# Four gate projections of the merge as filling work in the last delta head's scan, in place of two ahead of it

## Chip, cores and metric

The kernel runs on one core of one Trainium2 chip. The metric is the device time of one execution, in microseconds. Its engines here: PE (TensorE), DVE (VectorE), ACT (ScalarE), POOL (GpSimd) and SP (SyncE, which here only issues transfers). Each runs its own instructions strictly in order, and they wait for one another through semaphores.

## What is computed

One transformer block over 512 tokens of width 1024, with 256 context tokens ahead of them: a feed-forward sublayer, a mixer and a second feed-forward sublayer. The mixer has eight attention heads and eight gated delta-rule heads; both run over chunks and are merged:

```python
def step(s, xs):
    q_d, k_d, u_c, w_c, a_c, d_c = xs
    v_new = u_c - jnp.einsum('bhcd,bhde->bhce', w_c, s)
    o = jnp.einsum('bhcd,bhde->bhce', q_d, s) + jnp.einsum('bhij,bhje->bhie', a_c, v_new)
    s = s * d_c[..., None, None] + jnp.einsum('bhcd,bhce->bhde', k_d, v_new)
...
def _merge(o_dn, z, o_at, gates, dn_norm, w_dn_out, w_attn_out, w_out):
    o = _rmsnorm(jnp.swapaxes(o_dn, 1, 2), dn_norm).astype(z.dtype)
    o = o * jax.nn.silu(z.reshape(b, l, DN_HEADS, DN_DV))
    y_dn = o.reshape(b, l, DN_V) @ w_dn_out
    y_at = o_at @ w_attn_out
    g_dn, g_at = jnp.split(gates, 2, axis=-1)
    return (jax.nn.sigmoid(g_dn) * y_dn + jax.nn.sigmoid(g_at) * y_at) @ w_out
```

## The kernel before

Everything is held transposed: 128 features on the partitions, tokens along the row. A projection to 128 output features is one block `Blk(base, it, j)`: eight k tiles, and each product of fp32 numbers as three matmuls on numbers split in a high and a low part (hi x hi, lo x hi, hi x lo), 24 matmuls for the 512 tokens. Weights come by SP's transfers into a ring of four buffers `raw`. ACT rounds a block to `w_hi` (L954, `split`), DVE subtracts to get `w_lo` (L1784, `split_next`; for one block of each delta head POOL does, L869); `w_hi` and `w_lo` have two places, by the block's parity. A block's result lies in the PSUM bank of its parity (`bank`), and PE may overwrite it when `psum_read` says that it has been read. PE's count `gemm_done` grows with each finished block.

The attention outputs `o_at` and then the delta outputs `o_dn` (eight rows of 512 each, one for a head) are operands of the merge, so they are split as well: ACT rounds (`oat_hi` L1538, `odn_hi` L1706), DVE subtracts (`oat_lo` L2416, `odn_lo` L2649).

The eight delta heads run one after the other (`dn_head`, written for each engine; heads 1 to 6 are a loop, the last is written out with `final` set). On PE a head is: products of keys; projections; transposes; then, behind the inverse of the 16 x 16 diagonal blocks on DVE (L2518, L2522), which go out and back by transfers as `d_xc` (four issued by SP at L743, two by ACT at L1644) and are spread to `d_x` (L2545) in three groups, the solver: nine steps of `mid` and `grow` (L2713, out of `d_qu`), each with a copy `d_qu` on ACT (L1652) and a masked product `d_w` on DVE (L2561, L2573); then the scan over six chunks in two directions: `from_keys` (PE `d_st,d_c`), residual `d_rhs` on DVE (L2581), `solve` (PE `d_rhs,d_w`), `d_vn` on ACT (L1664), `to_state` (PE `d_vn,d_kd`), new state `d_st` on DVE (L2589, L2591), and beside them `out_state` (L3315) and `out_values` (PE `d_at,d_vn`). At its end DVE copies `d_o` (L2450).

In heads 0 to 6 the scan holds pieces of the next head's projections, of 384 columns each: `fill(n)` puts n matmuls there. The last head has none:

```python
def fill(n):
    if not final:
        piece(b[6], next_value, n)
```

Its blocks b[4] and b[5] are the two gates of the merge's first output tile. PE does 21 of b[5]'s 24 matmuls ahead of the solver and 3 before the last `grow`. ACT takes their sigmoids (`gate`, L1586) into `m_s`. Before each change between Ln/Exp, Silu and Sigmoid it loads the set of tables in which they are; the kernel asks for some of these loads (`preload_act_table_set`, L1624, L1636, L1660, L1703), others stand ahead of an instruction of their own (L1575, L1577, L1586).

Behind the scan the last head's output is normed: square, sum of squares on PE (`out_sum`, between attention rows 2 and 3 of the first merge projection, `attended`), Ln and Exp on ACT (`out_root`, L1575, L1577), `out_rows` on DVE. Then come `odn` and the merge loop: 8 output tiles of 4 blocks, gate of attention, gate of delta, attention, delta. The first tile lacks its two gates, so 7 tiles run in a loop of 96 matmuls. The matmuls of all of these are recorded on L2709.

## Time and profile before

| | |
|---|---|
| median of 3 runs | 1856.89 us (1856.65 to 1859.82) |
| profiled execution, its own time | 1859.1 us |
| its span | 1857.4 us |
| PE, DVE, ACT, POOL busy | 97%, 67%, 52%, 22% of the span |
| last delta head | about 1193 to 1251 us |
| merge loop (7 tiles) | 1270.7 to 1423.1 us |

Times in the rows are microseconds from the span's start. PE's busy share counts pipelined matmuls from start to end, which overlap, so it says little of how full PE is; the idle times in brackets, and the granted clock, say more.

### The profile page before, as it was taken

To read this page: it belongs to the slowest core of one execution; us is meant where nothing else is said; L and a number is where in the kernel's file an instruction comes from. 1 tells how busy PE (TensorE), PEld (TensorE's weight loads), DVE (VectorE), ACT (ScalarE), POOL (GpSimd) and SP (SyncE) were. 2 spreads that over 40 slices of the span, in tenths; PEclk is the share of its full clock that TensorE was granted. 3 is DMA by queue.
4 is the path that set the end of the run, shared out by engine and by line. 5 is a ranking of instruction groups with operands and counts; after the bars stand their busy time and mean duration, and the time that the engine had idled before them with its cause. 6 is when DMAs were issued, how large, how long until landed. Compare 5 with 4: busy or idle time off the path is not lost.

```text
span 1857.4 us, 31438 instructions
## 1 busy us (share of the span) xinstructions
PE 1792.7 (97%) x11197; PEld 1662.5 (90%) x11197; DVE 1239.0 (67%) x2451; ACT 956.9 (52%) x1912; POOL 401.2 (22%) x296
## 2 busy tenths in 40 slices
PE   8899999999998999999999999979999989999997
PEld 5899999999997889989999999967888989898897
DVE  7768787878667665567677787755334576376576
ACT  6534242424447655566556766644223565374463
POOL 0714141313200220023323222310000043242330
PEclk9999999999999999999999999989999999999999
DMA  8233334554231430031122222112324213233232
GB/s 331 73 119 134 122 123 141 180 175 154 88 140 41 154 102 13 1 88 52 46 67 76 65 76 65 45 38 68 99 93 169 69 47 114 70 113 103 85 131 69
DMA packets 85141, 182.86 MB, mean 98 GB/s; under 512 B 33572, under 2 KB 42916, under 8 KB 84912
## 3 DMA queue, kind: packets, MB, share of 16 engines
q1 hardware_dynamic: 79584, 167.45, 27.3%
q0 software_dynamic: 3280, 13.95, 2.3%
q8 instruction: 62, 1.02, 0.2%
q10 hardware_dynamic: 2176, 0.13, 0.1%
q14 instruction: 39, 0.32, 0.1%
HBM read 169.91 MB, written 7.39 MB: 95 GB/s over the span
## 4 chain that ended last, share of the span: by engine, by line
PE 73%; DVE 9%; ACT 6%; issue 4%; DMA 3%; SPq 3%; POOL 2%; ACTq 0%; DVEq 0%; POOLq 0%
PE ps L2709 50%; PE ps L2920 14%; PE ps L2713 3%; PE ps L3007 2%; SPq L737 2%; DMA raw<-W 1%; PE ps L3164 1%; ACT e_hi L1282 1%; DVE e_lo L2078 1%; DMA d_xc<-d_b 1%; ACT ps L1267 1%; PE ps L3315 1%; DMA d_matrices<-d_l 1%; DVE ps L2120 1%; DVE d_kc L2437 1%
## 5 line engine op out<-in xcount | busy, mean ns | idle before, releaser
L2709 PE MATMUL ps<-h_hi,w_hi 128*128 128x384 f32 (+2 forms) x720 | 240.4, 372 | 8.0 <-DVE h_lo L1854 4.1
L2709 PE MATMUL ps<-h_lo,w_hi 128*128 128x384 f32 (+2 forms) x720 | 237.0, 361 | 0.0
L2709 PE MATMUL ps<-h_hi,w_lo 128*128 128x384 f32 (+2 forms) x720 | 228.0, 356 | 0.0
L1784 DVE TENSOR_TENSOR w_lo<-raw,w_hi 128x1024 fp32r<-128x1024 f32 (+1 forms) x98 | 126.1, 1287 | 128.4 <-ACT w_hi L954 128.4
L954 ACT ACTIVATE w_hi<-raw 128x1024 fp32r<-128x1024 f32 (+1 forms) x106 | 111.4, 1051 | 153.6 <-PE ps L2709 151.7
L2709 PEld LDWEIGHTS ps<-h_hi,w_hi 128*128 128x128 f32 x720 | 130.5, 188 | 29.4 <-DVE h_lo L1854 8.2
L2709 PEld LDWEIGHTS ps<-h_lo,w_hi 128*128 128x128 f32 x720 | 133.1, 188 | 13.0 <-issue 1.2
L2709 PEld LDWEIGHTS ps<-h_hi,w_lo 128*128 128x128 f32 x720 | 133.0, 188 | 12.9
L2709 PE MATMUL ps<-g_hi,w_hi 128*128 128x384 f32 (+2 forms) x444 | 132.9, 346 | 0.8 <-DVE w_lo L1784 0.5
L2709 PE MATMUL ps<-g_lo,w_hi 128*128 128x384 f32 (+2 forms) x444 | 131.8, 343 | 0.0
L2709 PE MATMUL ps<-g_hi,w_lo 128*128 128x384 f32 (+2 forms) x444 | 131.7, 343 | 0.0
L2920 PE MATMUL ps<-h_lo,w_hi 128*128 128x384 f32 x320 | 107.0, 334 | 2.2 <-ACT pb L1212 2.2
L3007 PE MATMUL ps<-f_hi,e_hi 128*128 128x256 f32 x356 | 102.1, 287 | 6.0 <-ACT f_pb L1326 3.8
L2920 PE MATMUL ps<-h_hi,w_hi 128*128 128x384 f32 x320 | 107.3, 335 | 0.4 <-DVE ps L2008 0.3
L2920 PE MATMUL ps<-x_lo,w_hi 128*128 128x384 f32 x320 | 106.9, 334 | 0.0
L2920 PE MATMUL ps<-h_hi,w_lo 128*128 128x384 f32 x320 | 106.9, 334 | 0.0
L3007 PE MATMUL ps<-f_hi,e_lo 128*128 128x256 f32 x356 | 101.1, 284 | 0.0
L804 POOL TENSOR_TENSOR sums<-raw 128x512 f32<-128x512 f32 x20 | 28.9, 1444 | 278.6 <-DVE w_lo L1968 180.6
L2709 PEld LDWEIGHTS ps<-g_hi,w_hi 128*128 128x128 f32 x444 | 81.5, 188 | 7.4 <-DVE Y L2066 1.0
L2709 PEld LDWEIGHTS ps<-g_hi,w_lo 128*128 128x128 f32 x444 | 81.8, 188 | 5.0
L2709 PEld LDWEIGHTS ps<-g_lo,w_hi 128*128 128x128 f32 x444 | 81.7, 188 | 5.0
L1968 DVE TENSOR_TENSOR w_lo<-sums,w_hi 128x512 fp32r<-128x512 f32 x80 | 59.9, 753 | 33.8 <-ACT w_hi L1172 33.0
(479 smaller groups left out, 5134.1 us busy)
## 6 DMA issues: line engine op xcount, KB each, us to landing
raw<-W SPq DMA_DIRECT2D x221, 512.0 KB, 3.8
w_mod<-WMOD SPq DMA_DIRECT2D x68, 512.0 KB, 4.0
g_row<-g_rows POOLq DMA_DIRECT2D x8, 768.0 KB, 5.3
X<-XT SPq DMA_DIRECT2D x4, 768.0 KB, 6.9
d_matrices<-d_l SPq DMA_DIRECT2D x8, 384.0 KB, 2.8
a_sw<-i_n POOLq DMA_DIRECT2D x40, 64.0 KB, 1.9
w_first<-WMOD SPq DMA_DIRECT2D x4, 512.0 KB, 11.0
X<-XT SPq DMA_DIRECT2D x1, 2048.0 KB, 14.2
```

The costliest lines, as they stand in the source:

```text
L737: sp.dma_start(d_s[lv][r:r + b, :, col:col + b], d_l[r:r + b, 0, :, col:col + b]).then_inc(s("d_levels"), 16)
L804: g.tensor_tensor(s1[:], b1, b2, ALU.add).then_inc(s("s_add"), 1)
L954: a.activation(hi, src, ACT.Copy).then_inc(s("w_hi"), 1)
L1267: a.activation(copy_bank(pos), weight_part2(q, pos), ACT.Copy)
L1282: a.activation(slot2(True, q, pos), weight_part2(q, pos), ACT.Copy).then_inc(s("u_hi"), 1)
L1784: v.tensor_tensor(lo, src, hi.bitcast(F32), ALU.subtract).then_inc(s("w_split"), 1)
L1968: v.tensor_tensor(slot_of(w_lo, n, None), weight_part(q, pos), slot_of(w_hi, n, None).bitcast(F32), ALU.subtract)\
L2078: v.tensor_tensor(slot2(False, q, pos), src, slot2(True, q, pos).bitcast(F32), ALU.subtract).then_inc(s("u_lo"), 1)
L2709: return pe.matmul(out, lhsT, rhs, start=start, stop=stop)
L2713: return pe.matmul(out, lhsT, rhs, start=False, stop=True, skip_group_check=True)
L2920: last = pe.matmul(out_, slot_of((w_hi, w_hi, w_lo)[i], n + pos, k), (hi, lo, hi)[i][pos][:, k], start=pos in (A11, A12, S3) and k == 0 an ...
L3007: last = pe.matmul(out_, w[i][:, k], (hi, lo, hi)[i][:, k], start=pos in (A11, A12, S3) and k == 0 and i == 0, stop=True, skip_group_check ...
```

## The change

Blocks b[6] and b[7] of the last head, which were the attention and delta projection of the first tile, become the two gates of the second tile; the host puts the weight blocks in that order (`mg[0:8]`), and `merge_block` gives the place of a block in it. The four gates' results go to `m_gate`, two of them in new places.

On PE all of b[5] comes ahead of the solver, and four matmuls of b[6] behind it; `fill` puts 8, 4 or 2 gate matmuls where the other heads have 12, 5 or 3 of theirs, so that 34 stand between the last `grow` and the scan's end, and 10 behind it. On ACT the first gate is read with a Copy, and its sigmoid and the second gate follow the transfer of `d_xc`. The third gate is in step 3 of the scan, the fourth behind the scan. The attention rows are taken in the order 3 to 7, 0 to 2 (`ROWS`; the buffers of rows 0 to 2 are still in use in the scan): five are rounded in steps 1, 2 and 4 and split in steps 2, 3 and 4. The splits of the weights of the first tile's projections come in steps 3 (ACT) and 5 (DVE) and behind the scan. The second tile's projections are written out like the first's, and the merge loop has 6 tiles.

```diff
@@ -245,6 +245,16 @@
         return Blk(self.base, self.it, self.j + d)
+def merge_block(it, j):
+    if isinstance(it, int) and it < 2:
+        return Blk(B_MERGE, 0, 2 * it + j + (2 if j >= 2 else 0))
+    return Blk(B_MERGE, it, j)
+ROWS = list(range(3, H)) + list(range(3))
@@ -393,6 +403,7 @@
         m_s = at("m_s", 94, [2, SEQ])
+        m_gate = [m_s[:, 0, :], m_s[:, 1, :], at("m_s2", 98, [SEQ])[:], at("m_s3", 87.4375, [SEQ])[:]]
@@ -1533,8 +1544,8 @@
-            def round_attention(k0, k1):
-                for k in range(k0, k1):
+            def round_attention(i0, i1):
+                for k in ROWS[i0:i1]:
@@ -1581,9 +1592,9 @@
-            def gate(blk, i):
+            def gate(blk, to, bank_):
                 a.wait_ge(s("gemm_done"), blk.n + 1)
-                a.activation(m_s[:, i, :], bank(blk, 1), ACT.Sigmoid).then_inc(psum_read[blk.pair], 1)
+                a.activation(to, bank_, ACT.Sigmoid).then_inc(psum_read[blk.pair], 1)
@@ -1633,9 +1644,9 @@
                 if final:
-                    a.preload_act_table_set(SIGMOID_SET)
                     a.wait_ge(s("d_qd"), h + 1)
-                    gate(b[4], 0)
+                    a.wait_ge(s("gemm_done"), b[4].n + 1)
+                    a.activation(m_gate[0], bank(b[4], 1), ACT.Copy).then_inc(psum_read[b[4].pair], 1)
@@ -1646,6 +1657,11 @@
                     distance(h + 1, 1)
+                else:
+                    a.preload_act_table_set(SIGMOID_SET)
+                    a.wait_ge(psum_read[b[4].pair], b[4].turn + 2)
+                    a.activation(m_gate[0], m_gate[0], ACT.Sigmoid)
+                    gate(b[5], m_gate[1], bank(b[5], 1))
@@ -1655,9 +1671,6 @@
                     take(b[5])
-                else:
-                    gate(b[5], 1)
-                    a.preload_act_table_set(LOG_SET)
@@ -1666,6 +1679,13 @@
                         split(b[7])
+                    if final and t in (1, 2):
+                        round_attention(2 * t - 2, 2 * t)
+                    if final and t == 3:
+                        gate(b[6], m_gate[2], ps[:, 0, :])
+                        split(b[6].ahead(2))
+                    if final and t == 4:
+                        round_attention(4, 5)
@@ -1694,28 +1714,32 @@
                 a.activation(m_hi[:, bass.ds(it, 1), :].rearrange("p a n -> p (a n)"), m_b[:], ACT.Copy).then_inc(s("m_rounded"), 1)
+            last_gate = Blk(B_MERGE, 0, 3)
             out_square(H - 1)
-            round_attention(0, 2)
+            round_attention(5, 7)
             out_round(H - 1, 1)
-            round_attention(2, 4)
+            round_attention(7, H)
+            gate(last_gate, m_gate[3], bank(last_gate, 1))
+            split(last_gate.ahead(2))
+            a.preload_act_table_set(LOG_SET)
             out_root(H - 1)
-            round_attention(4, H)
...
                 a.activation(odn_hi[:, k], o_dn[:, k], ACT.Copy).then_inc(s("o_rounded"), 1)
-            step(Blk(B_MERGE, 0, 2))
-            step(Blk(B_MERGE, 0, 3))
-            merged(0)
+            for it in range(2):
+                step(merge_block(it, 2))
+                step(merge_block(it, 3))
+                merged(it)
...
                     if j < 2:
-                        gate(blk, j)
+                        gate(blk, m_s[:, j, :], bank(blk, 1))
                 merged(it)
-            with a.Fori(1, KT, 1) as it:
+            with a.Fori(2, KT, 1) as it:
@@ -2410,9 +2434,9 @@
-            def split_attention(k0, k1):
-                for k in range(k0, k1):
-                    v.wait_ge(s("o_rounded"), k + 1)
+            def split_attention(i0, i1):
+                for i, k in list(enumerate(ROWS))[i0:i1]:
+                    v.wait_ge(s("o_rounded"), i + 1)
@@ -2600,8 +2624,14 @@
                         pack(h + 1)
+                    if final and t in (2, 3):
+                        split_attention(2 * t - 4, 2 * t - 2)
+                    if final and t == 4:
+                        split_attention(4, 5)
...
                         out_rows(h - 1)
+                    if final and t == 5:
+                        split_next(b[6].ahead(2))
@@ -2620,23 +2650,23 @@
             dn_head(H - 1, False, True)
-            split_attention(0, 1)
+            split_attention(5, 6)
             out_add(H - 1)
-            split_attention(1, 3)
+            split_attention(6, 7)
...
             out_gain(H - 1)
-            split_attention(3, H)
+            split_attention(7, H)
+            split_next(Blk(B_MERGE, 0, 5))
...
-            def gated(blk, dst, i):
-                gate = blk.ahead(-2)
+            def gated(blk, dst, row, gate):
...
                 v.wait_ge(s("gemm_done"), blk.n + 1)
-                v.tensor_tensor(dst[:], bank(blk, 1), m_s[:, i, :], ALU.mult).then_inc(psum_read[blk.pair], 1)
-            def merged_sum(it):
-                v.wait_ge(psum_read[Blk(B_MERGE, it, 3).pair], Blk(B_MERGE, it, 3).turn + 2)
+                v.tensor_tensor(dst[:], bank(blk, 1), row, ALU.mult).then_inc(psum_read[blk.pair], 1)
+            def merged_sum(blk):
+                v.wait_ge(psum_read[blk.pair], blk.turn + 2)
@@ -2647,23 +2677,27 @@
                 v.tensor_tensor(odn_lo[:, k], o_dn[:, k], odn_hi[:, k].bitcast(F32), ALU.subtract).then_inc(s("o_split"), 1)
-            gated(Blk(B_MERGE, 0, 2), m_b, 0)
-            split_next(Blk(B_MERGE, 0, 4))
-            gated(Blk(B_MERGE, 0, 3), m_a, 1)
-            merged_sum(0)
-            step(Blk(B_MERGE, 0, 3))
-            merged_low(0)
+            for it in range(2):
+                gate = Blk(B_MERGE, 0, 2 * it + 1)
+                if it:
+                    v.wait_ge(s("m_ready"), it)
+                gated(merge_block(it, 2), m_b, m_gate[2 * it], gate)
+                split_next(merge_block(it, 2).ahead(2))
+                gated(merge_block(it, 3), m_a, m_gate[2 * it + 1], gate)
+                merged_sum(merge_block(it, 3))
+                split_next(merge_block(it, 3).ahead(2))
+                merged_low(it)
...
                     if j >= 2:
-                        gated(blk, (m_b, m_a)[j - 2], j - 2)
+                        gated(blk, (m_b, m_a)[j - 2], m_s[:, j - 2, :], blk.ahead(-2))
                     if j == 3:
-                        merged_sum(it)
+                        merged_sum(blk)
...
                 merged_low(it)
-            with v.Fori(1, KT, 1) as it:
+            with v.Fori(2, KT, 1) as it:
@@ -3173,7 +3207,7 @@
                 hi, lo, off = ((h_hi, h_lo, 0), (h_hi, h_lo, 0), (oat_hi, oat_lo, CTX), (odn_hi, odn_lo, CTX))[j]
-                gemm(Blk(B_MERGE, it, j), hi, lo, segs_x, off=off, ready=(s("o_split"), H * (j - 2)) if j >= 2 else None)
+                gemm(merge_block(it, j), hi, lo, segs_x, off=off, ready=(s("o_split"), H * (j - 2)) if j >= 2 else None)
@@ -3241,13 +3275,29 @@
+                gates = [(blk, bank_, k, i) for blk, bank_ in ((b[6], ps[:, 0, :]), (b[7], bank(b[7], 1))) for k in range(KT) for i in range(3)]
+                def gate_piece(n):
+                    for _ in range(n):
+                        blk, bank_, k, i = gates.pop(0)
+                        if k == 0 and i == 0:
+                            pe.wait_ge(s("w_split"), blk.w + 1)
+                            pe.wait_ge(psum_read[blk.pair], blk.turn + 1)
+                        w, x = ((w_hi, h_hi), (w_hi, h_lo), (w_lo, h_hi))[i]
+                        last = mm(bank_, w[:, blk.pair, k, :], x[:, k, CTX:T], k == 0 and i == 0, k == KT - 1 and i == 2)
+                        if k == KT - 1 and i == 2:
+                            last.then_inc(s("gemm_done"), 1)
...
                         piece(b[6], next_value, n)
+                    else:
+                        gate_piece({12: 8, 5: 4, 3: 2}[n])
...
                 if final:
-                    query(b[5], 0, KT - 1)
+                    query(b[5], 0, KT)
+                    gate_piece(4)
@@ -3321,9 +3371,7 @@
                             .then_inc(s("sc_o"), 1)
-                if final:
-                    query(b[5], KT - 1, KT)
-                else:
+                if not final:
@@ -3353,6 +3401,8 @@
                 out_values(NCH - 1)
+                if final:
+                    gate_piece(len(gates))
@@ -3362,26 +3412,28 @@
-            def attended(k0, k1):
-                blk = Blk(B_MERGE, 0, 2)
-                if k0 == 0:
+            def attended(i0, i1):
+                blk = merge_block(0, 2)
+                if i0 == 0:
...
                     pe.wait_ge(psum_read[blk.pair], blk.turn + 1)
-                for k in range(k0, k1):
-                    pe.wait_ge(s("o_split"), k + 1)
+                for i0_, k in list(enumerate(ROWS))[i0:i1]:
+                    pe.wait_ge(s("o_split"), i0_ + 1)
                     for i, (w, x) in enumerate(((w_hi, oat_hi), (w_hi, oat_lo), (w_lo, oat_hi))):
-                        last = mm(bank(blk, 1), w[:, blk.pair, k, :], x[:, k], k == 0 and i == 0, k == KT - 1 and i == 2)
-                if k1 == KT:
+                        last = mm(bank(blk, 1), w[:, blk.pair, k, :], x[:, k], i0_ == 0 and i == 0, i0_ == KT - 1 and i == 2)
+                if i1 == KT:
                     last.then_inc(s("gemm_done"), 1)
-            attended(0, 3)
+            attended(0, 7)
             out_sum(H - 1, 1)
-            attended(3, KT)
+            attended(7, KT)
             merge_gemm(0, 3)
+            merge_gemm(1, 2)
+            merge_gemm(1, 3)
...
                     merge_gemm(it, j)
-            with pe.Fori(1, KT, 1) as it:
+            with pe.Fori(2, KT, 1) as it:
@@ -3483,8 +3535,10 @@
                    _tiles(i["w_dn_out"][0])], 1)
+    mg = mg.reshape(-1, P, D)
+    mg[0:8] = mg[[0, 1, 4, 5, 2, 3, 6, 7]]
     W = np.concatenate(_ffn1_blocks(i["ffn1_w_gu"][0], i["ffn1_w_down"][0])
-                       + [_tiles(pad), _tiles(w_kv)[0:HKV], _tiles(w_q), _tiles(w_kv)[HKV:], dn.reshape(-1, P, D), mg.reshape(-1, P, D),
+                       + [_tiles(pad), _tiles(w_kv)[0:HKV], _tiles(w_q), _tiles(w_kv)[HKV:], dn.reshape(-1, P, D), mg,
```

**ACT, last head, from the tables of the key norms (`k_sum`) to the solver's copies (`d_qu`).** Before:

```order
L1634 ACTIVATE d_q_153<-d_c 128x512
L1636 ACT_TABLE_LOAD
L1586 ACTIVATE m_s<-ps 128x512
L954 ACTIVATE w_hi<-raw 128x1024
L1575 ACT_TABLE_LOAD
L1575 ACTIVATE d_os<-ps,small 128x512
L1577 ACT_TABLE_LOAD
L1577 ACTIVATE o_dn<-d_os 128x512
L1644 DMA d_xc<-d_b 128x1x16 x2
L1652 ACTIVATE d_qu<-ps 128x256 x3
```

Now:

```order
L1645 ACTIVATE d_q_153<-d_c 128x512
L1649 ACTIVATE m_s<-ps 128x512
L965 ACTIVATE w_hi<-raw 128x1024
L1586 ACTIVATE d_os<-ps,small 128x512
L1588 ACTIVATE o_dn<-d_os 128x512
L1655 DMA d_xc<-d_b 128x1x16 x2
L1661 ACT_TABLE_LOAD
L1663 ACTIVATE m_s<-m_s 128x512
L1597 ACTIVATE m_s<-ps 128x512
L1668 ACTIVATE d_qu<-ps 128x256 x3
```

Three loads ahead of the transfer are gone; one load and both sigmoids follow it.

**PE, last head, step 3 of the scan** (`from_keys`, `out_values`, `solve`, `out_state`, `to_state`, and what follows). Before:

```order
L2709 MATMUL ps<-d_st,d_c 128x128 x2
L2713 MATMUL ps<-d_at,d_vn 128x128 x2
L2709 MATMUL ps<-d_rhs,d_w 128x128 x2
L3315 MATMUL ps<-d_qd,d_st 128x128 x2
L2709 MATMUL ps<-d_vn,d_kd 128x128 x2
```

Now:

```order
L2743 MATMUL ps<-d_st,d_c 128x128 x2
L2747 MATMUL ps<-d_at,d_vn 128x128 x2
L2743 MATMUL ps<-d_rhs,d_w 128x128 x2
L3365 MATMUL ps<-d_qd,d_st 128x128 x2
L2743 MATMUL ps<-d_vn,d_kd 128x128 x2
L2743 MATMUL ps<-h_hi,w_lo 128x512
L2743 MATMUL ps<-h_hi,w_hi 128x512
L2743 MATMUL ps<-h_lo,w_hi 128x512
L2743 MATMUL ps<-h_hi,w_lo 128x512
```

Four matmuls of the fourth gate (`h_hi` and `h_lo` are the normed input) follow each such step.

## Rows read from the trace of the kernel before

**Rows 1.** The page, section 4: shares of the chain that ended last.

```profile
PE 73%; DVE 9%; ACT 6%; issue 4%; DMA 3%; SPq 3%; POOL 2%; ACTq 0%; DVEq 0%; POOLq 0%
```

**Rows 2.** The chain (start, us, what); groups by line, 1270.6 to 1426 (busy, mean ns | idle before, releaser).

```profile
1270.66 152.64 PE ps L2709 x672
...
L954 ACT ACTIVATE w_hi<-raw 128x1024 fp32r<-128x1024 f32 x29 | 30.8, 1061 | 110.6 <-PE ps L2709 110.6
```

**Rows 3.** The chain in order of time, last head, before the solver.

```profile
1208.67 1.28 ACT L1636
...
1211.52 1.28 ACT L1575
...
1214.21 4.19 DMA d_xc<-d_b
```

**Rows 4.** Timelines of SP and ACT, last head (start, us, engine, line, what [idle before]).

```profile
1211.31 2.69 SPq L743 DMA_DIRECT2D d_xc<-d_b  x4
...
1213.54 1.34 ACTq L1644 DMA_DIRECT2D d_xc<-d_b  x2
...
1232.17 1.28 ACT L1660 ACT_TABLE_LOAD   x1
...
1233.46 0.45 ACT L1664 ACTIVATE d_vn<-ps 128x128 f32<-128x128 f32 x2
```

**Rows 5.** Timelines of PE, ACT and DVE behind the scan.

```profile
1253.41 0.76 PE L2709 MATMUL ps<-oat_hi,w_hi 128*128 128x512 f32 x1 [2.78 <-DVE oat_lo L2416]
...
1261.13 0.50 PE L2709 MATMUL ps<-oat_hi,w_hi 128*128 128x512 f32 x1 [1.45 <-DVE oat_lo L2416]
...
1264.73 0.47 PE L2709 MATMUL ps<-odn_hi,w_hi 128*128 128x512 f32 x1 [0.57 <-DVE odn_lo L2649]
...
1261.93 1.28 ACT L1703 ACT_TABLE_LOAD   x1
...
1263.89 4.91 DVE L2649 TENSOR_TENSOR odn_lo<-o_dn,odn_hi 128x512 fp32r<-128x512 f32 x8 [0.41 <-ACT odn_hi L1706]
...
1269.32 1.21 DVE L1784 TENSOR_TENSOR w_lo<-raw,w_hi 128x1024 fp32r<-128x1024 f32 x1
```

**Rows 6.** Stretches: length, busy of PE, PEld, DVE, ACT, POOL, then PEclk, DMA, GB/s.

```profile
1235.00:1243.00 8.00, 7.74 (x32) 6.33 (x32) 2.83 (x9) 2.05 (x5) 2.36 (x1) 0.57 0.14 39
...
1253.00:1260.00 7.00, 6.26 (x14) 4.37 (x14) 4.03 (x7) 3.22 (x7) 0.00 (x0) 0.54 0.01 2
```

**Rows 7.** Timelines of SP, DVE and PE in the head before (head 6).

```profile
1156.60 2.72 SPq L743 DMA_DIRECT2D d_xc<-d_b  x4
...
1160.63 1.10 DVE L2545 TENSOR_TENSOR d_x<-d_xc,ca 128x256 f32<-128x256 f32 x3 [0.82 <-DMA d_xc<-d_b]
...
1172.12 0.61 PE L2713 MATMUL ps<-d_qu 128*128 128x128 f32 x4
...
1176.60 0.61 PE L2709 MATMUL ps<-d_st,d_c 128*128 128x128 f32 x4
...
1192.94 0.69 DVE L2450 COPY d_o<-ps 128x512 f32<-128x512 f32 x1 [1.62 <-PE ps L2713]
```

**Rows 8.** Timelines of DVE and PE in the last head.

```profile
1218.43 0.76 DVE L2545 TENSOR_TENSOR d_x<-d_xc,ca 128x256 f32<-128x256 f32 x2 [3.21 <-DMA d_xc<-d_b]
...
1230.59 0.61 PE L2713 MATMUL ps<-d_qu 128*128 128x128 f32 x4
...
1234.80 0.71 PE L2709 MATMUL ps<-d_st,d_c 128*128 128x128 f32 x4 [0.23 <-DVE d_st L2589]
...
1250.67 0.69 DVE L2450 COPY d_o<-ps 128x512 f32<-128x512 f32 x1 [0.87 <-PE ps L2713]
```

**Rows 9.** Timelines of ACT, DVE and POOL in the last head's scan.

```profile
1243.93 0.54 ACT L1664 ACTIVATE d_vn<-ps 128x128 f32<-128x128 f32 x2 [3.03 <-PE ps L2709]
...
1244.87 0.61 DVE L2591 SCALAR_TENSOR_TENSOR d_st<-d_st,hc,ps 128x128 f32<-128x128 f32 x2 [1.25 <-PE ps L2709]
...
1238.29 2.36 POOL L869 TENSOR_TENSOR w_lo<-raw,w_hi 128x1024 fp32r<-128x1024 f32 x1 [12.00 <-ACT w_hi L954]
```

## The prediction

> **What bounds the kernel now.** I first read the page's chain by engine, then the chain in order of time around the last delta head, then each engine's timeline there, and last the same timelines of the head before it, whose scan already has filling matmuls.
>
> PE holds 73% of the chain [rows 1]. The merge loop behind the last head is one unbroken PE piece, 672 matmuls in 152.64 us, 0.2271 us each [rows 2]. So a matmul that leaves this loop takes 0.227 us off the end, unless it costs something where it goes.
>
> In the last head the chain runs through all engines, and PE waits in it at four places. (1) Before the solver it waits for the second and third `d_x`, at 1218.43, which wait for the transfer of `d_xc` that ACT issued at 1213.54. The inverse which that transfer reads was done earlier: SP, released by the same count, issued its own part at 1211.31. ACT was late because of table loads, at 1208.67 for the gate, and from 1211.52 on two more, back to logarithm and exponential [rows 3, 4]. (2) After the solver PE waits for the first `d_vn`, at 1233.46; ACT does a load, the second gate and another load ahead of it [rows 4]. (3) After the scan PE waits 2.78 us for the first `oat_lo`, and (4) again 1.45 and 0.57 us while ACT rounds four more rows and loads the sigmoid set [rows 5]. After the waits of (2) and (3) the granted clock falls from 2.4 to 1.2 GHz: it is 0.57 on average from 1235 to 1243, in the scan, and 0.54 from 1253 to 1260, where 14 matmuls of 512 columns take 6.26 us, 0.45 each [rows 6].
>
> **The change, part by part**, against the profiled execution's own 1859.1 us.
>
> *The merge loop.* Two gate projections of 24 matmuls leave it: 48 x 0.227 = **-10.9 us**. ACT and DVE don't bound the loop: ACT's 29 splits there wait for PE 110.6 us in total [rows 2]. The weight blocks in their new order are still read one after the other: nothing.
>
> *Start of the solver.* The first gate becomes a Copy, so the logarithm set stays. Without three loads of 1.28 us ACT is through with `out_root` near 1211.5, and issues its two transfers near 1211.1, as soon as the inverse is done. What then happens the head before shows: SP issues at 1156.60, and all three `d_x` follow in one run of 1.10 us from 1160.63, 4.03 us behind that issue [rows 7]. Here SP issues at 1211.31, so they end at 1211.31 + 4.03 + 1.10 = 1216.44 instead of 1218.43 + 0.76 = 1219.19 [rows 8]: **-2.75**. PE meanwhile does seven matmuls more (three of the second gate, four of the third), 1.6 us, which this wait of PE hides still; were it gone, they would cost just that. The load of the sigmoid set and two sigmoids (2.5 us on ACT) lie between the transfer and the solver, where ACT has nothing else.
>
> *The solver.* From the end of `d_x` to the start of the last `grow` the head before needs 1172.12 - 1161.73 = 10.39 us [rows 7], the last head 1230.59 - 1219.19 = 11.40 [rows 8]. Three matmuls ahead of that `grow` go too, so I take 10.2: **-1.2**. The last `grow` is then at 1226.65.
>
> *Into the scan.* From there to the first product with the state: now 1234.80 - 1230.59 = 4.21 [rows 8], with ACT's loads in it. In the head before 1176.60 - 1172.12 = 4.48 [rows 7], with 18 fills of 384 columns, at three quarters of 0.227 some 3.1 us. The change has 12 of 512 columns, 2.7 us: 4.1, **-0.1**.
>
> *The scan.* From there to the copy `d_o`: now 1250.67 - 1234.80 = 15.87, almost half of it at the low clock [rows 6, 8]. The head before takes 1192.94 - 1176.60 = 16.34 [rows 7] with 30 fills (5.1 us) and a convolution on DVE. The change has 22 fills (5.0 us) and no convolution, for which I take half a microsecond off (an estimate, between 0 and its whole length). ACT gets five roundings, a gate and a split (4.3 us together); they fit into its waits, which are 3.03 us in a step [rows 9]. DVE gets five splits of a row, 0.6 each, between `d_rhs` and `d_st`, where it waits 1.25 us in a step [rows 9] (two take 1.2), and one of a weight (1.2) behind the last `d_rhs`. Not covered: the fourth gate waits for POOL's `w_lo`. ACT's split ends near 1233.9, POOL takes 2.36 [rows 9], so 1236.3, and PE could start at 1236.0: 0.3. Sum 15.9: **0.0**. `d_o` starts near 1246.7 instead of 1250.67, -4.0 in all.
>
> *After the scan*, counted from `d_o`. PE does the last 10 gate matmuls and 21 of the rows, of which five are ready: 31 x 0.227 = 7.0, then the sum of squares, out at 7.75. By then ACT has done the fourth gate, a split and the load of the logarithm set (until 7.3). Ln and Exp end at 9.1, the sigmoid load at 10.4, and the first odn matmul comes as far behind that load as now, 1264.73 - 1263.21 = 1.5: 11.9, against 14.06 now [rows 5, 8]. The next block of the merge waits for DVE's `w_lo`, which ends 1270.53 - 1263.89 = 6.64 us behind the start of the first `odn_lo` [rows 5]: 17.8, now 20.0. That alone is -2.2. But PE's waits have moved together: from 8.3 to 11.9 it is idle, 3.6 us, longer than the 2.78 after which the clock fell [rows 5, 6]. A fall like that one (0.54 over 7 us, so 6.4 us low) costs half its length where PE is full, 3.2, less the 0.4 that PE would have waited: +2.8. Bounds are 0 and 3.2; I take 2.6, near the upper, as this is the longest wait of the stretch: **+0.4** together.
>
> Sum: -10.9 - 2.75 - 1.2 - 0.1 + 0.0 + 0.4 = -14.55, so 1844.5 from the profiled execution. The median of the runs shown, 1856.89, is 2.2 below that execution; from it the sum gives 1842.3. Low-clock stretches may well differ between executions, and the change removes two of them; I predict halfway: **1843.4 us**.
>
> *A rule against a row.* In this trace a table load keeps ACT for 1.28 us and the next instruction follows at once: load at 1232.17, `d_vn` at 1233.46 [rows 4]. The Trainium skill (ScalarE: Activation LUTs, section What ACT_TABLE_LOAD costs) adds a drain of about 1.38 us to each switch to another set; by that rule the two loads behind the scan, between the fourth gate and the first odn rounding, would cost 1.38 more each and the sum would be some 2 us worse. The row decides here.
>
> **The rivals.**
>
> *The clock holds behind the scan.* For it: PE is dense up to the wait, and after the wait of 1.45 us the next long piece ran at 0.227 [rows 2, 5]. Then -14.55 - 2.6 = -17.15: 1841.9 by the execution's own time, 1839.7 by the median. Chance 0.2.
>
> *The scan has less room than the head before suggests.* The clock falls once in it, or ACT's and DVE's new pieces come ahead of `d_vn` and `d_st`. A low stretch of 6.4 us costs 3.2 on a PE that is now full; a DVE split late by its own 0.6 in three steps costs 1.8. Together +5: 1849.5. For it: DVE has 1.25 us for 1.2 us of work [rows 9]. Chance 0.17.
>
> *The transfer isn't earlier*, because SP's own last part, issued near 1213.4, lands no sooner than ACT's did: the 2.75 stay, 1847.3. Against it are the rows of the head before. Chance 0.08.
>
> *A table load has a pause behind it* that shows only before some instructions. The rows leave 0.01 us [rows 4]. Were it as long as the load, 1.28 twice behind the scan: +2.6, 1847.1. This is where the rule above would act. Chance 0.03.
>
> *Slower: the chain through the scan carries all that is put in.* Each engine takes its instructions strictly in turn, and PE, ACT and DVE wait for one another in every step. Between the last `grow` and `d_o` are added 34 matmuls (7.7 us, at 0.45 each 15.3), 4.3 us on ACT and 4.2 on DVE. All exposed and at the low clock that is +23.8, against -10.9 - 4.0 + 0.4 for the rest: +9.3, 1868.4. It turns the sign from 14.5 us of exposed work on. Against it: the head before carries 48 fills there and takes 20.8 us from its last `grow` to `d_o`, the last head without any 20.1 [rows 7, 8]. Chance 0.04.
>
> That the change doesn't do what it says can be left out: the order of PE's instructions has 38 matmuls of the third and fourth gate before the scan's end and 10 behind it.
>
> **How the numbers follow.** The forecast has 0.48, the rivals 0.2, 0.17, 0.08, 0.03 and 0.04. The range goes from the case in which the clock holds, by the median, 1839.5, to just below that of a tight scan, 1849. About 0.2% (3.7 us) is what a measurement of this kernel can tell from no change. All cases but the last are beyond it; 0.03 stays for a scan still tighter than I price it. Faster 0.93, same 0.03, slower 0.04.
>
> **What would show it.** In the changed profile: one PE piece of 624 matmuls in 141.7 us; no table load between 1207.5 and ACT's transfer; three `d_x` in one run that ends near 1216.4; `d_o` near 1246.7; the clock full through solver and scan and low once behind it; the first odn matmul 11.9 us behind `d_o`. The prediction would be wrong by steps of the scan beyond 3.4 us, a PE wait for `w_lo` of over 1 us, or a `d_vn` queued behind ACT's gate or roundings.

## The result, and the profile after

Four runs of the changed kernel have a median of **1843.47 us** (1840.84 to 1844.51), beside 1858.36 (1856.65 to 1861.58, four runs) for the kernel before: ratio 0.9912, 95% interval 0.99 to 0.9925. The change makes the kernel 0.9% faster. The forecast was 1843.4.

The two profiled executions are 1857.4 and 1841.4 us long, 16.0 apart. I cut them at the same events as the forecast did; each column is counted from the one before it, and the last is what follows from the next block of the merge to the end of the span.

| us | SP issues `d_xc` at | `d_x` end | last `grow` | first `from_keys` | `d_o` | first odn matmul | next block | rest |
|---|---|---|---|---|---|---|---|---|
| before | 1211.31 | 7.88 | 11.40 | 4.21 | 15.87 | 14.06 | 5.93 | 586.7 |
| forecast | 1211.31 | 5.13 | 10.2 | 4.1 | 15.9 | 11.9 | 8.5 | 575.8 |
| after | 1210.10 | 4.57 | 10.32 | 4.22 | 17.11 | 11.70 | 7.16 | 576.2 |

(The forecast's next block is 17.8 + 2.6 = 20.4 behind `d_o`, and its rest 586.7 - 10.9.) The first column moves between executions of one kernel as well: over all the runs below it lies between 1208.38 and 1211.13. From that issue to the next block it was 59.35 us before and is 55.08 now. This stretch holds all that the change does outside the merge loop, and I compare the runs by it. It comes from one profiled execution of each kernel. What follows it has a scatter of its own: with nearly the same instructions in it the rest is between 574.2 and 578.2 us in the runs below, so the medians, which have some 2 us of spread, can't order the single edits.

**The merge loop.** The page's chain, then the chain behind the last head (start, us, what), then the groups of 1264 to 1406, answering to [rows 1, 2]:

```profile
PE 75%; DVE 8%; ACT 6%; issue 4%; POOL 2%; DMA 2%; SPq 2%; ACTq 0%; DVEq 0%; POOLq 0%
```

```profile
1261.91 144.89 PE ps L2743 x638
```

```profile
L965 ACT ACTIVATE w_hi<-raw 128x1024 fp32r<-128x1024 f32 x26 | 27.6, 1061 | 99.5 <-PE ps L2743 99.5
```

Still one unbroken piece at 144.89 / 638 = 0.2271 each. It holds the end of the odn matmuls too, hence 638 and not 624. The piece ends at 1406.80, so from the next block at 1265.18 on the 624 take 141.6 us, 11.0 less than the 672 before.

**Start of the solver**, timelines of SP, ACT and DVE (start, us, engine, line, what), answering to [rows 3, 4, 8]:

```profile
1209.99 1.29 ACTq L1655 DMA_DIRECT2D d_xc<-d_b  x2
1210.10 2.83 SPq L754 DMA_DIRECT2D d_xc<-d_b  x4
1211.32 1.28 ACT L1661 ACT_TABLE_LOAD   x1 [0.97 <-issue]
...
1213.43 1.24 DVE L2569 TENSOR_TENSOR d_x<-d_xc,ca 128x256 f32<-128x256 f32 x3 [2.17 <-DMA d_xc<-d_b]
```

ACT issues its part 0.11 us ahead of SP and loads the table behind it. All three `d_x` come in one run.

**The scan.** Two places of the chain in order of time, from the second and the fourth step:

```profile
1232.47 0.61 DVE d_rhs L2605 x2
1233.08 2.60 DVE oat_lo L2440 x2
1235.68 0.27 DVE d_st L2615
...
1240.69 0.54 ACT d_vn L1677 x2
1241.22 0.53 ACT oat_hi L1549
...
1241.77 0.69 DVE oat_lo L2440
1242.46 0.27 DVE d_st L2615
```

The row splits are on the chain twice. The timelines of DVE and POOL say more: two `oat_lo` take 2.69 us together, where two others take 1.28, and POOL makes its `w_lo` at that time.

```profile
1233.00 2.69 DVE L2440 TENSOR_TENSOR oat_lo<-o_at,oat_hi 128x512 fp32r<-128x512 f32 x2
...
1237.05 1.28 DVE L2440 TENSOR_TENSOR oat_lo<-o_at,oat_hi 128x512 fp32r<-128x512 f32 x2
...
1241.77 0.69 DVE L2440 TENSOR_TENSOR oat_lo<-o_at,oat_hi 128x512 fp32r<-128x512 f32 x1 [1.41 <-ACT oat_hi L1549]
...
1232.16 2.37 POOL L880 TENSOR_TENSOR w_lo<-raw,w_hi 128x1024 fp32r<-128x1024 f32 x1 [10.69 <-ACT w_hi L965]
```

The first four steps, from one `from_keys` to the next, take 2.82, 3.96, 3.34 and 3.45 us; without the row splits, in an experiment below, they take 2.82, 3.11, 3.24 and 3.23.

**Behind the scan**, timelines of ACT and PE, answering to [rows 5]:

```profile
1252.15 1.28 ACT L1724 ACT_TABLE_LOAD   x1
1253.85 0.69 ACT L1586 ACTIVATE d_os<-ps,small 128x512 f32<-128x512 f32 x1 [0.42 <-PE ps L2743]
1254.57 0.63 ACT L1588 ACTIVATE o_dn<-d_os 128x512 f32<-128x512 f32 x1
1255.22 1.28 ACT L1726 ACT_TABLE_LOAD   x1
1256.51 4.27 ACT L1729 ACTIVATE odn_hi<-o_dn 128x512 fp32r<-128x512 f32 x8
...
1258.02 0.47 PE L2743 MATMUL ps<-odn_hi,w_hi 128*128 128x512 f32 x1 [3.50 <-DVE odn_lo L2679]
```

PE waits once, for 3.50 us. The stretches, with the granted clock third from the end, answer to [rows 6]:

```profile
1231.00:1239.00 8.00, 7.26 (x51) 6.20 (x50) 6.75 (x14) 5.22 (x12) 2.37 (x1) 1.00 0.20 66
1239.00:1246.30 7.30, 7.25 (x52) 6.47 (x51) 4.16 (x9) 2.01 (x6) 0.00 (x0) 1.00 0.01 2
...
1258.00:1265.20 7.20, 7.18 (x25) 5.75 (x26) 5.81 (x9) 3.74 (x7) 0.00 (x0) 0.76 0.06 10
```

The clock is full through the scan and at 1.2 GHz for 3.4 us behind the wait.

### The profile page after: what moved, and what is told of

Its sections match the earlier page's. It is cut to its first block, busy times and chain, and to the rows that moved or that the text cites. A ratio compares the mean times of both kernels' runs of the same rounds, so it can differ in the third digit from the quotient of the medians.

```text
span 1841.4 us, 31413 instructions
## 1 busy us (share of the span) xinstructions
PE 1785.0 (97%) x11197; PEld 1657.5 (90%) x11197; DVE 1239.0 (67%) x2451; ACT 952.5 (52%) x1910; POOL 400.8 (22%) x296
## 4 chain that ended last, share of the span: by engine, by line
PE 75%; DVE 8%; ACT 6%; issue 4%; POOL 2%; DMA 2%; SPq 2%; ACTq 0%; DVEq 0%; POOLq 0%
PE ps L2743 52%; PE ps L2954 15%; PE ps L2747 3%; PE ps L3041 2%; DMA raw<-W 1%; SPq L748 1%; PE ps L3198 1%; ACT e_hi L1293 1%; DVE e_lo L2102 1%; ACT ps L1278 1%; DVE ps L2144 1%; DVE d_kc L2461 1%; PE ps L3327 1%; PE ps L3365 1%; DMA d_matrices<-d_l 0%
## 6 DMA issues: line engine op xcount, KB each, us to landing
w_first<-WMOD SPq DMA_DIRECT2D x4, 512.0 KB, 10.9
```

## The experiments

All but the last two were timed in three to five rounds beside the kernel before. The first four shared one chip, on which the kernel before took 1858.72; the next four another, where it took 1859.47. The last two were run once, with a profile, beside 1856.18.

| run | median us | ratio, interval | issue of `d_xc` to next block | scan, `from_keys` to `d_o` | `d_o` to first odn | low clock behind the scan |
|---|---|---|---|---|---|---|
| r_again | 1845.58 | 0.9921 (0.9905 to 0.9938) | 56.31 | 17.11 | 11.66 | 6.8 |
| r_old_table | 1845.61 | 0.993 (0.9914 to 0.9947) | 58.93 | 17.10 | 11.66 | 3.4 |
| r_no_fill | 1845.96 | 0.9934 (0.9918 to 0.9951) | 59.47 | 15.79 | 19.41 | 3.4 |
| r_rows_behind | 1843.4 | 0.9919 (0.9902 to 0.9935) | 55.10 | 15.83 | 14.55 | 3.4 |
| r_splits_later | 1840.18 | 0.9906 (0.989 to 0.9923) | 54.86 | 15.83 | 11.68 | 6.8 |
| r_busy_wait | 1842.47 | 0.9908 (0.9892 to 0.9925) | 53.79 | 17.11 | 11.70 | none |
| r_one_set | 1840.8 | 0.9904 (0.9887 to 0.992) | 53.71 | 17.11 | 10.32 | 3.4 |
| r_all_three | 1836.82 | 0.9882 (0.9865 to 0.9898) | 49.35 | 15.83 | 8.53 | none |
| r_pool_two_inputs | 1843.18 (one) | | 54.89 | 17.00 | 11.67 | 3.4 |
| r_pool_no_input | 1839.32 (one) | | 53.82 | 15.84 | 11.68 | 3.4 |

### The changed kernel again

No edit: what does one execution differ from another by?

> The changed kernel once more, as the yardstick for the runs beside it. Expected 1843.5 us, within 2 us. In its profile: the two oat_lo in step 2 of the last head's scan take 2.7 us instead of 1.3 where they meet POOL's w_lo, the clock falls once behind the scan, PE waits 3.5 us for the first odn_lo. If the clock's fall depends on how the wait lies to the chip, it may be somewhat longer or shorter than the 3.4 us of the first profile.

The stretch is 56.31 here and 55.08 in the first profile. The median, 1845.58, is 2.1 us above the first four runs', just outside what I expected. Every part of the stretch agrees within 0.25 us but one: from the first odn matmul to the next block 8.23 against 7.16, where the low clock lasts 6.8 us instead of 3.4. So only with equal low-clock stretches are two profiles comparable to some 0.2 us.

### The transfer: the table loads ahead of it put back

```diff
                 if final:
+                    a.preload_act_table_set(SIGMOID_SET)
                     a.wait_ge(s("d_qd"), h + 1)
-                    a.wait_ge(s("gemm_done"), b[4].n + 1)
-                    a.activation(m_gate[0], bank(b[4], 1), ACT.Copy).then_inc(psum_read[b[4].pair], 1)
+                    gate(b[4], m_gate[0], bank(b[4], 1))
```

> One part undone: the first gate is taken as a sigmoid in its old place, with the load of the sigmoid set and the two loads back to Ln and Exp ahead of ACT's transfer of d_xc; everything else as in the changed kernel. My theory: ACT's transfer is issued 2.5 us later, the second and third d_x come apart from the first and end 3 us later (counted from SP's first issue: 7.9 instead of 4.6), and all that follows moves with them: 3 us slower, 1846.5. PE then waits about 4.5 us ahead of the solver in two pieces, and if the clock falls there another 0.5 to 1 us. Rival (the transfer is bound by SP's own last part): d_x ends where it did, within 0.5 us, and the time is that of the changed kernel.

ACT's and DVE's timelines of this run:

```profile
1209.77 1.28 ACT L1586 ACT_TABLE_LOAD   x1
...
1211.77 1.28 ACT L1588 ACT_TABLE_LOAD   x1
1211.79 1.36 ACTq L1655 DMA_DIRECT2D d_xc<-d_b  x2
...
1216.07 0.76 DVE L2567 TENSOR_TENSOR d_x<-d_xc,ca 128x256 f32<-128x256 f32 x2 [3.13 <-DMA d_xc<-d_b]
```

The picture of [rows 3, 4, 8] is back: ACT issues 2.24 us behind SP (1209.55), two `d_x` wait 3.13 us, and they end 7.28 us behind SP's issue instead of 4.57. The solver goes back to 11.49 from 10.32, and the clock is low for 3.4 us at its start (1217.4 to 1220.8). The clock fell there in the kernel before too, a third fall beside the two that the prediction names. Stretches of its solver, the granted clock third from the end:

```profile
1220.00:1221.00 1.00, 1.00 (x7) 1.00 (x6) 1.00 (x4) 0.08 (x1) 0.00 (x0) 0.50 0.00 0
...
1222.00:1223.00 1.00, 1.00 (x11) 1.00 (x10) 0.62 (x1) 0.34 (x2) 1.00 (x1) 1.00 0.00 0
```

So what the solver gained belongs to the wait ahead of it, and little of it to the three matmuls. The stretch is 3.85 us longer than the changed kernel's with an equal low clock behind the scan (58.93 against 55.08): 2.7 from the transfer and 1.2 from the solver. The median doesn't show it, 1845.61 beside 1845.58 for the unedited kernel on the same chip, where I had expected 1846.5.

### The fills: the 34 gate matmuls behind the scan

```diff
                         piece(b[6], next_value, n)
-                    else:
-                        gate_piece({12: 8, 5: 4, 3: 2}[n])
```

The third gate, and the splits of weights that go with it, move behind the scan as well.

> The 34 gate matmuls between the last grow and the end of the scan are done behind the scan instead (44 there, ahead of the attention rows), with the third gate's reading and both weight splits behind it; rows still rounded and split in the scan. It measures what the scan hides. My theory (most of them lie in waits): from the last grow to d_o it takes 4 us less at full clock (17 instead of 21), up to 2 less saving if the clock falls in the scan, and the 7.7 us of matmuls come back behind d_o: 4 to 6 us slower than the changed kernel, 1847.5 to 1849.5. Rival (the chain through the scan carries all that is put in): 7.7 us less there, 7.7 more behind: same time as the changed kernel.

The first `from_keys` comes 2.46 us behind the last `grow` (with fills 4.22), the scan takes 15.79 (17.11), and the sum of squares is issued 14.58 us behind `d_o` (6.87). So 34 matmuls cost 7.7 us behind the scan, 34 x 0.227, and 1.76 + 1.32 = 3.1 us where the change put them: 4.6 of the 7.7 are hidden. Of the 12 ahead of the first `from_keys`, 2.7 us, two thirds are exposed; of the 22 in the scan, 5.0 us, a quarter. I had expected 4 us less from the last `grow` to `d_o`, and it is 3.1. The stretch is 4.4 us longer (59.47 against 55.08), as long as it was before the change (59.35); the median, 1845.96, is only 0.4 above the unedited kernel's on the same chip, and below the 1847.5 to 1849.5 expected.

The quarter needs a warning. This run still has the slow row splits in its scan, and its steps are 2.72, 4.12, 2.79 and 3.55 us, the last part 2.61, against 2.82, 3.96, 3.34, 3.45 and 3.54 in the changed kernel. In the two steps that wait for a slow split the fills cost nothing; all of their cost is in the others. With 2.79 for each step that a split held up the scan would take 13.7, an estimate from these steps. Without a slow split but with the fills it takes 15.83 (below). So beside well placed splits the fills would cost some 2.1 of their 5.0 us. The kernel before needs 15.87 without any, but with its clock low for almost half of that.

### The rows: all eight split behind the scan, as before

```diff
-ROWS = list(range(3, H)) + list(range(3))
+ROWS = list(range(H))
...
-                    if final and t in (1, 2):
-                        round_attention(2 * t - 2, 2 * t)
...
-                    if final and t in (2, 3):
-                        split_attention(2 * t - 4, 2 * t - 2)
```

> The other part undone: no attention row is rounded or split in the scan, all eight behind it in the old order around the norm of the last output (0, 1 | 2, 3 | 4 to 7); the four gates stay filling. My theory: the scan gets shorter by about 1.2 us, for the splits that meet POOL's w_lo and the one that waits for ACT's rounding are gone, but behind the scan four roundings (2.1 us) stand again between the norm and the sigmoid load, and the sum of squares comes as early as the rows allow: first odn matmul 12.5 to 13.5 us behind d_o instead of 11.7; together within 1 us of the changed kernel, 1843 to 1845. Rival (the rows in the scan were what saved 2 us behind it and cost nothing in it): 2 us slower, 1845.5 or more.

PE's sum of squares goes back behind three rows with them, as in the kernel before. The scan is 1.28 us shorter, the first odn matmul comes 2.85 later behind `d_o` (14.55, where I had expected 12.5 to 13.5), and the stretch is the same, 55.10 against 55.08 at an equal length of low clock. So the five rows in the scan, as the change put them, bring nothing: they cost 1.3 us in the scan, and of the 2.85 that they give back behind it 1.7 goes, since PE's waits are then one long one, the low clock behind it falls on the odn matmuls, and the next block comes 7.16 instead of 5.44 us behind the first of them.

### The row splits one step later

```diff
-                    if final and t in (2, 3):
-                        split_attention(2 * t - 4, 2 * t - 2)
-                    if final and t == 4:
-                        split_attention(4, 5)
+                    if final and t in (3, 4):
+                        split_attention(2 * t - 6, 2 * t - 4)
...
                     if final and t == 5:
+                        split_attention(4, 5)
                         split_next(b[6].ahead(2))
```

> DVE's five row splits stand in scan steps 3, 4 and after the last step's d_rhs instead of in steps 2, 3 and 4, so none runs while POOL makes w_lo of the first gate split. Theory (two engines get in each other's way: DVE's splits of two fp32 operands take three to four times as long beside POOL's subtraction): every oat_lo takes about 0.69 us, the second step of the scan takes 3.1 instead of 3.96 us, and d_o starts 15.9 to 16.3 us behind the first product with the state instead of 17.1. Rival (mere queueing, a split is late by its own length wherever it stands): the second step gets shorter and a later one longer by as much, d_o stays near 17.1. Time: about 1 us below the changed kernel by the stretch from SP's issue to the merge's next block, which the runs' median may not show.

The same eight splits by tile (count: shortest, median, longest in ns):

```profile
L2440 DVE TENSOR_TENSOR oat_lo<-o_at,oat_hi x8: 679/683/692, 1234.4 to 1248.5; 128x512 fp32r<-128x512 f32 x8
```

None is slow, the second step takes 3.11 us, the scan 15.83, with the five splits still in it. The third and fourth step take 3.24 and 3.23, no more than without any row split. So DVE does have room for two splits in a step, as forecast [rows 9]. Of the 1.28 us that the scan lost, 0.85 was in the second step, with the split beside POOL's `w_lo`, 0.22 in the fourth, with the one that waited for ACT's rounding behind `d_vn`, and 0.1 each in the third step and behind the fifth `from_keys`. The stretch is 1.45 below the repeated run's, which had the same 6.8 us of low clock.

### POOL beside DVE

The order of the last experiment, in which nothing is slow, with work on POOL behind its `w_lo`, across the first two splits: once two multiplications with two inputs from SBUF, once four fills with zero. Their results are read by nobody.

```diff
                 next_low(7)
+                if final:
+                    for i in range(2):
+                        g.tensor_tensor(d_vtok[:], d_vtok[:], off_mask[:].unsqueeze(1).to_broadcast([P, NCH, P]), ALU.mult).then_inc(s("lvl"), 1)
+                        g.wait_ge(s("lvl"), h + 2 + i)
```

> The order with the row splits one step later (every oat_lo 0.69 us), with two multiplications of 128x768 floats on POOL behind its w_lo, from SBUF into a buffer that nobody reads; POOL's own such operation took 1.8 us in this kernel, so POOL is busy some 3.6 us longer, across the first two oat_lo (1234.4 to 1235.6 in the run without it). Theory (the two engines block each other when both read SBUF): one of those two oat_lo, which took 0.69 us each, now takes 1.5 to 2.5 us, d_st behind them is late by that, and the step grows by 0.7 us or more. Rival (what was slow in the changed kernel was the place in the order, not POOL): both stay at 0.69 us and the scan at 15.8 us.

> The same order with four fills of 128x768 floats with zero on POOL in the same place, which write SBUF and read nothing. Theory that only reading of SBUF by POOL stands in DVE's way: every oat_lo stays at 0.69 us and the scan at 15.8 us. Theory that any work of POOL on SBUF does: at least one oat_lo takes over 1.2 us.

Timelines of POOL and DVE and the splits by tile, first with the multiplications:

```profile
1234.45 4.10 POOL L910 TENSOR_TENSOR d_vtok<-d_vtok,off_mask 128x768 f32<-128x768 f32 x2
...
1236.06 3.04 DVE L2444 TENSOR_TENSOR oat_lo<-o_at,oat_hi 128x512 fp32r<-128x512 f32 x2
```

```profile
L2444 DVE TENSOR_TENSOR oat_lo<-o_at,oat_hi x7: 679/685/2339, 1236.1 to 1249.3; 128x512 fp32r<-128x512 f32 x7
```

then with the fills:

```profile
1232.99 3.12 POOL L910 MEMSET d_vtok<- 128x768 f32 x4
...
1234.62 1.28 DVE L2444 TENSOR_TENSOR oat_lo<-o_at,oat_hi 128x512 fp32r<-128x512 f32 x2
```

One split takes 2.34 us instead of 0.68 beside the multiplications, the third step 4.30 instead of 3.24, the scan 17.00 instead of 15.83. Beside the fills nothing changes. So it is POOL, not the place in the order, and of POOL's two kinds of work only the one that reads SBUF did it. Each was run once, and a fill and a multiplication differ in more than the reading; that it is the reading rests on the page named next. The Trainium skill (SBUF — State Buffer, section SBUF: two separate sides) states just this: the two engines share one pair of SBUF ports, under an exclusive lock; a DVE operation with two SBUF inputs is held up by a POOL operation that reads SBUF, and the loser waits for the whole of it. The runs agree on which operations are held up: 1.40 us of wait in the changed kernel (2.08 - 0.68), 1.66 with the multiplications, none beside the fills. `d_rhs`, which takes one of its inputs from PSUM, kept its 0.61 for two at 1232.47 beside POOL's `w_lo`. The runs don't show a wait for the whole: in the changed kernel the first of the two splits ran at full speed within the recorded span of POOL's `w_lo`, and the second ended 1.16 us behind its end. That stays open; POOL's recorded start and end may not be those of its reading.

### The wait behind the scan: filled

```diff
             attended(7, KT)
+            for _ in range(13):
+                mm(ps[:, 6, :], h_hi[:, 1, 0:P], h_hi[:, 0, CTX:T])
             merge_gemm(0, 3)
```

> Thirteen matmuls of 512 columns on operands that lie ready, into a bank that nobody reads, stand in PE's order between the sum of squares and the first odn matmul; they fill 3.0 of the 3.5 us in which PE waits there. Theory (the clock falls behind that wait because PE is idle in it): the granted clock stays at 1.00 behind the scan, the odn matmuls take 5.5 us instead of 7.2, and the merge's next block starts 17.4 to 17.8 us behind d_o instead of 18.9 to 19.9, so 1.1 to 2.5 us come back. Rival (the fall belongs to the place in the program or to something else than this wait): it falls as before and the next block starts at 18.9 or later.

PE's timeline, then the stretch from the first odn matmul on:

```profile
1253.77 3.12 PE L2743 MATMUL ps<-h_hi 128*128 128x512 f32 x13
1257.43 0.47 PE L2743 MATMUL ps<-odn_hi,w_hi 128*128 128x512 f32 x1 [0.55 <-DVE odn_lo L2679]
```

```profile
1257.30:1264.00 6.70, 6.40 (x27) 5.04 (x28) 6.67 (x11) 4.70 (x8) 0.00 (x0) 1.00 0.00 0
```

The first odn matmul comes as before, 11.70 behind `d_o`, but the clock stays at 2.4 GHz and the next block follows after 5.86 us, against 7.16 and 8.23 in the two profiles of the changed kernel. So the clock's fall is worth 1.3 us (3.4 us low) or 2.4 (6.8 us low), and it comes of PE's idle wait. The median, 1842.47, can't show so little.

### ACT: no table load behind the scan

```diff
-                        gate(b[6], m_gate[2], ps[:, 0, :])
+                        keep(b[6], m_gate[2], ps[:, 0, :])
...
-            gate(last_gate, m_gate[3], bank(last_gate, 1))
+            keep(last_gate, m_gate[3], bank(last_gate, 1))
             split(last_gate.ahead(2))
-            a.preload_act_table_set(LOG_SET)
             out_root(H - 1)
-            a.preload_act_table_set(SIGMOID_SET)
```

`keep` is the change's own trick for the first gate, a Copy; the two sigmoids follow the odn roundings.

> The third and fourth gate are read off PSUM by a Copy and their two sigmoids are taken behind the first odn rounding, so ACT loads no table between the scan's end and the logarithm and exponential; the logarithm set is loaded in an idle stretch of the scan. Theory (ACT's chain of gate, split, two loads, Ln, Exp sets the first odn matmul): it comes 1.3 us earlier, about 10.4 instead of 11.7 us behind d_o, and the next block 17.4 to 18.0 instead of 18.9 behind d_o. Rival (PE's own sum of squares, issued 6.9 us behind d_o, and DVE's chain behind it set it): the first odn matmul stays at 11.2 or later.

The first odn matmul is 1.34 us earlier behind `d_o` (10.32 after 11.66), one table load of 1.28. The other load was hidden behind PE's sum of squares. PE's wait is shorter:

```profile
1255.40 0.47 PE L2751 MATMUL ps<-odn_hi,w_hi 128*128 128x512 f32 x1 [2.16 <-DVE odn_lo L2687]
```

and the clock falls all the same.

### Three edits together

Row splits one step later, no table load behind the scan, and the sum of squares ahead of four rows instead of one:

```diff
-            attended(0, 7)
+            attended(0, 4)
             out_sum(H - 1, 1)
-            attended(7, KT)
+            attended(4, KT)
```

> Three edits together: row splits one step later, no table load on the way out of the scan, and the sum of squares ahead of the last four rows' matmuls (the same matmuls as before, in another order), so that it is issued about 2 us earlier. If ACT's loads and PE's order are what the way out of the scan is made of, then d_o is 1 us earlier, the first odn matmul starts 8.8 to 9.5 us behind d_o (now 11.7), the next block 14.8 to 16 (now 18.9 to 19.9), PE waits in two pieces of under 2.5 us and the clock need not fall: 3.5 to 5 us off the changed kernel, about 1839. If the time is set elsewhere (DVE's own roundings), the first odn matmul stays above 11 and the gain below 1.5 us.

Timelines of ACT and PE:

```profile
1250.24 0.68 ACT L1586 ACTIVATE d_os<-ps,small 128x512 f32<-128x512 f32 x1
1250.95 0.63 ACT L1588 ACTIVATE o_dn<-d_os 128x512 f32<-128x512 f32 x1
1251.49 4.27 ACT L1732 ACTIVATE odn_hi<-o_dn 128x512 fp32r<-128x512 f32 x8
...
1253.05 0.47 PE L2750 MATMUL ps<-odn_hi,w_hi 128*128 128x512 f32 x1 [0.36 <-DVE odn_lo L2686]
```

The root follows ACT's split without a pause, the first odn matmul comes 8.53 us behind `d_o`, PE waits 0.36 us for it and the clock holds. The stretch is 49.35 us, 5.7 less than the changed kernel's, and the median 1836.82: ratio to the kernel before 0.9882 (0.9865 to 0.9898), below the changed kernel's interval of 0.99 to 0.9925. It beats both kernels. Of the 5.7 us, 1.3 is the scan, 3.2 the earlier first odn matmul, of which the table load alone gave 1.3, and 1.3 the clock. The remaining 1.8 of the 3.2 came with the earlier sum of squares, which was not run by itself. The first odn matmul and the next block, 14.39 us behind `d_o`, come even a little earlier than I had expected.

## Why the prediction was right, and which step of it failed

*The merge loop, -10.9.* The piece is 11.0 us shorter and runs at 0.2271. Right. The whole rest behind the next block is 10.5 us shorter, but scatters by 4 us between executions.

*Start of the solver, -2.75.* Right in its mechanism, shown by the run with the old table loads; measured -3.3 and -3.1 in the two profiles of the changed kernel (4.57 and 4.78 behind SP's issue, not 5.13). The head before, from which the 5.13 came, was a little slow for it.

*The solver, -1.2.* Measured -1.08. It came back with the transfer's delay (11.49), with a short fall of the clock: the wait ahead of the solver was the greater part of its cause. I had the size from the head before, without seeing why that head's solver is shorter, and named only the matmuls.

*Into the scan, -0.1.* Measured 0.0. That two thirds of these fills are exposed (1.76 of 2.7 us) was in the term, since it took the head before with its own fills as the pattern.

*The scan, 0.0: this step failed.* It is +1.24 (17.11 against 15.87). The prediction gave DVE "five splits of a row, 0.6 each, between `d_rhs` and `d_st`, where it waits 1.25 us in a step", and priced each from its own duration alone. The room was as stated, but two of the places were not: one pair stands beside POOL's `w_lo`, where a split takes 2.08 us, and the fifth waits 1.41 us for its rounding, which ACT has queued behind `d_vn`. Moved by one step, the same five cost nothing, and the scan takes 15.83, the 15.9 forecast. The trace of before had the first of these to show. In the head before, DVE's product for the convolution stands beside POOL's `w_lo` (by tile, 1170 to 1200, and POOL's timeline):

```profile
L2437 DVE SCALAR_TENSOR_TENSOR d_kc<-d_up,hn,d_kc x2: 1015/1668/2321, 1180.5 to 1184.2; 128x770 f32<-128x770 f32 x2
```

```profile
1179.60 2.38 POOL L869 TENSOR_TENSOR w_lo<-raw,w_hi 128x1024 fp32r<-128x1024 f32 x1 [5.63 <-ACT w_hi L954]
```

One of two equal operations took 2.32 us, the other 1.02. I had taken "half a microsecond off" for the missing convolution and not looked at why its parts differ. The rival of a tight scan named the late split, with the wrong cause and, at +5, four times too large; the clock did not fall in the scan. One of the signs of being wrong that the prediction names was there, steps of the scan beyond 3.4 us: the second took 3.96 and the fourth 3.45.

*After the scan, +0.4.* The first odn matmul, 11.9 forecast, came at 11.70 and 11.66. PE's wait, 3.6 forecast, was 3.50. For the fall of the clock I took 2.6; the two profiles give 1.3 and 2.4, against the run in which it holds. With it the term measured -1.1 and -0.1. The mechanism was right, the size is that of an execution, not of the kernel.

*The table load's pause.* There is none: the load at 1255.22 takes 1.28 us, and `odn_hi` starts at 1256.51, 0.01 us behind its end. The Trainium skill (ScalarE: Activation LUTs, section What ACT_TABLE_LOAD costs) would add about 1.38 us; the trace does not agree, and it decides.

From SP's issue on, the terms sum to -14.55 as forecast and -14.8 as measured; of the 16.0 us between the two spans the last 1.2 lie ahead of this point, where the change alters nothing, within the scatter of the other runs. So the sum is good to 0.3 us, but with an error of +1.2 in the scan against -0.6 for the transfer and -1.5 behind the scan, nearly all of it the clock in that execution, and +0.6 in the small terms and the rest. That 1843.4 met 1843.47 is luck in another way too: I had put it halfway between two starting points by a guess, the kernel before came out at 1858.36 and not 1856.89, and the changed kernel, run again, took 1845.58.

## What to carry to other kernels

A free slot on an engine is free only for what can run in it: before putting an operation there, look for what the other engines do in that slot, and in the trace for the same operation with two different durations. A wait that you gather from several short ones into a long one can cost TensorE its clock just where it is then full, and an earlier start may be lost to it. When a filler is taken from one place and hidden in another, price both places: here two thirds of the matmuls ahead of the scan were exposed, and a quarter of those in it, where slow splits hid some of the others.

## What the runs showed of the hardware that I had not expected

DVE's subtraction of two SBUF operands of 128x512 floats took 0.68 us alone and 2.08 to 2.34 beside a POOL operation that reads SBUF; beside POOL's fills it took 0.68. Whether POOL is slowed in turn stays open: of the two multiplications of 128x768 floats one took 1.84 us and the other, beside both splits, 2.18, against 1.82 in the solver of the same run, but its `w_lo` took 2.37 beside the splits and 2.38 without. The low clock behind one and the same wait of 3.50 us lasted 3.4 us in some executions and 6.8 in others, which makes 1.1 us between two profiles of one kernel; behind a wait of 2.16 us it fell too, and with that wait at 0.36 us, in the run with three edits, it did not.
